# First blocks of a blocked triangular inverse: transposed on VectorE and moved by GpSimd instead of by TensorE products and ScalarE copies

## The reference, cut to what matters

```
def step(s, inp):
    r_t, w_t, k_t, v_t, kk_t, a_t = inp
    sa = jnp.einsum('bhvk,bhk->bhv', s, -kk_t)
    s = (s * w_t[:, :, None, :] + sa[..., None] * (kk_t * a_t)[:, :, None, :]
         + v_t[..., None] * k_t[:, :, None, :])
    return s, jnp.einsum('bhvk,bhk->bhv', s, r_t)
```

## Time and profile before

| | |
|---|---|
| Median of 3 runs | 3548.14 us (3544.28 to 3554.76) |
| Profiled execution | 3553.18 us, span 3551.4 us |
| PE, PEld, DVE, ACT, POOL busy | 3318.0, 2872.8, 2133.4, 766.6, 390.9 us |
| The scan's group loops | 181.4 to about 889 us, in four pieces (one for each pair) of about 108 us |
| L1109 and L1113, each | 36 times (4 pairs, 9 groups; pairs and groups are counted from 0) |

### The profile page before, as it was taken

How to read it: one execution, slowest core, us unless ns; L and a number is a source line. 1 busy time by engine, 2 the same in 40 slices (tenths; PEclk the granted TensorE clock), 3 DMA queues, 4 the chain that set the end, 5 groups by cost and what they waited for, 6 DMA issues and landing times.

```text
span 3551.4 us, 155986 instructions
## 1 busy us (share of the span) xinstructions
PE 3318.0 (93%) x72354; PEld 2872.8 (81%) x72354; DVE 2133.4 (60%) x3890; ACT 766.6 (22%) x1815; POOL 390.9 (11%) x536
## 2 busy tenths in 40 slices
PE   7989899898999999299999999999999999999997
PEld 3486767768455545299999999999999999999997
DVE  4566657676344444666666666666666665666665
ACT  3445344444244443000000000000000000000002
POOL 0141524334211000000000000000000000000001
PEclk9999999999999999699999999999999999999999
DMA  8200000000311113398989998988989989899996
GB/s 359 72 6 9 18 10 17 5 20 5 99 33 33 44 54 108 130 326 287 292 280 292 289 287 281 291 288 279 284 282 287 289 285 284 277 288 291 284 288 210
DMA packets 570778, 671.25 MB, mean 189 GB/s; under 512 B 56942, under 2 KB 463750, under 8 KB 567054
## 3 DMA queue, kind: packets, MB, share of 16 engines
q1 hardware_dynamic: 564430, 641.85, 55.5%
q0 software_dynamic: 5520, 19.34, 2.6%
q10 hardware_dynamic: 176, 0.05, 0.0%
HBM read 631.68 MB, written 28.30 MB: 186 GB/s over the span
## 4 chain that ended last, share of the span: by engine, by line
PE 56%; issue 1%; SPq 1%; DVE 1%; DMA 0%; ACT 0%; DVEq 0%
PE banks L2555 34%; PE banks L2580 20%; PE banks L2496 2%; SPq L2403 1%; SPq L2410 0%; DMA e_wgu<-in_e_up 0%; DVE e_wd L2859 0%; DVE e_wgu L2859 0%; SPq L2413 0%; DVE e_wgu L2928 0%; DVE e_xe L2917 0%; DVE e_wsum L2757 0%; ACT e_xp L2695 0%; ACT e_xT L2695 0%; DVE e_wgu L2762 0%
## 5 line engine op out<-in xcount | busy, mean ns | idle before, releaser
L2580 PE MATMUL banks<-e_hid,e_wd 128*64 128x144 f32 x11264 | 1280.4, 286 | 12.3 <-issue 9.5
L2580 PEld LDWEIGHTS banks<-e_hid,e_wd 128*64 128x64 f32 x11264 | 782.4, 137 | 15.6 <-issue 15.2
L2555 PE MATMUL banks<-e_xsum,e_wgu 128*64 128x72 f32 x11264 | 518.8, 226 | 12.2 <-issue 12.2
L2555 PE MATMUL banks<-e_xsum,e_wsum 128*64 128x72 f32 x11264 | 523.1, 226 | 7.2 <-issue 5.5
L2555 PE MATMUL banks<-e_xT,e_wgu 128*64 128x72 f32 x11264 | 519.1, 226 | 10.5 <-issue 9.2
L2555 PEld LDWEIGHTS banks<-e_xT,e_wgu 128*64 128x64 f32 x11264 | 501.3, 137 | 14.3 <-issue 14.2
L2555 PEld LDWEIGHTS banks<-e_xsum,e_wsum 128*64 128x64 f32 x11264 | 503.4, 137 | 8.9 <-issue 7.0
L2555 PEld LDWEIGHTS banks<-e_xsum,e_wgu 128*64 128x64 f32 x11264 | 498.7, 137 | 14.1 <-issue 14.0
L2790 DVE TENSOR_TENSOR e_gu<-e_first,banks 128x288 f32<-128x288 f32 x176 | 79.9, 454 | 676.2 <-ACT e_first L2676 507.5
L2676 ACT ACTIVATE e_first<-banks 128x144 f32<-128x144 f32 x176 | 51.4, 292 | 1416.4 <-PE banks L2555 1416.4
L2555 PE MATMUL banks<-e_xT,e_wsum 128*64 128x72 f32 x5632 | 257.7, 226 | 1.5 <-issue 1.3
(11 more groups left out here) (399 smaller groups left out, 4815.6 us busy)
## 6 DMA issues: line engine op xcount, KB each, us to landing
e_wgu<-in_e_gate SPq DMA_DIRECT2D x704, 256.0 KB
e_wgu<-in_e_up SPq DMA_DIRECT2D x704, 256.0 KB
e_wd<-in_e_down SPq DMA_DIRECT2D x704, 256.0 KB, 4.0
h_wmod<-in_w_mod SPq DMA_DIRECT2D x24, 1024.0 KB, 16.8
wblk<-in_w_in SPq DMA_DIRECT2D x22, 512.0 KB, 14.6
h_x<-in_x_sample SPq DMA_DIRECT2D x8, 512.0 KB, 7.1
wo<-in_w_out SPq DMA_DIRECT2D x2, 2048.0 KB, 11.9
scratch_ffn<-hT_x SPq DMA_DIRECT2D x8, 512.0 KB, 5.1
```

Source lines behind the costliest of these rows:

```text
L2555: last = nc.tensor.matmul(bank[4 + 2 * (n % 2) + g][c, q * HT:(q + 1) * HT], a[:, k, c], b[:, k, :], start=(k == 0), stop=(k == HALF - 1))
L2580: last = nc.tensor.matmul(bank[k // PER_BANK][c, at:at + TOK], wd[n % WD][:, b, k * P + h * CH:k * P + (h + 1) * CH], hid[n % 2][:, b, :], ...
```

## The change

PE's twelve products and ScalarE's two copies are gone. DVE's new `first_T(g)` makes the transposes, two `transpose` instructions of 128 x 128 that transpose each 32x32 block by itself; they stand in DVE's queue just ahead of `level(g, 1)`. The move to the other half is made by a masked sum that is written straight into the other half, twice 64 partitions: by GpSimd at the end of `first_inverse` for groups 1 to 8, by DVE in `inverse_start` for group 0. `w1_ok` counts these halves, and PE's `level_Y(g, 1)` waits for it.

```diff
-                    def inverse_start(g):
-                        pages.wait(w0_ok, p * GR + g + 1)
...
-                                    last = pages.matmul(bank[5][f, at:at + CH],
-                                                            W0[f, i, :] if d else TW[g % 2][f, d, 1, i, :],
-                                                            K.idc[f, :], start=True, stop=True)
-                        last.then_inc(t0ps, 1)
-                    def inverse_copy(g):
...
-                                last = pages.matmul(bank[6][HS[h], at:at + CH], K.idc[f, :], W0[f, i, :],
-                                                        start=True, stop=True)
-                        last.then_inc(w_cps, 1)
...
                             if d and lev == 1:
-                                pages.wait(w_cok, p * GR + g + 1)
+                                pages.wait(w1_ok, p * (2 * GR) + 2 * g + 2)
...
-                        act.wait_ge(t0ps, p * GR + g + 1)
...
-                        act.wait_ge(w_cps, p * GR + g + 1)
...
+                        pool.wait_ge(w0_ok, p * GR + g + 1)
+                        for h in range(2):
+                            f = FAR[1][h]
+                            nc.gpsimd.tensor_tensor(TW[g % 2][HS[h], 1, 1, :, :], N0[f, 1, :, :], eye[f], ALU.add)\
+                              .then_inc(w1_ok, 1)
+                            pool.wait_ge(w1_ok, p * (2 * GR) + 2 * g + h + 1)
...
+                        for h in range(2):
+                            f = FAR[1][h]
+                            V.tensor_tensor(TW[g % 2][HS[h], 1, 1, :, :], N0[f, 1, :, :], eye[f], ALU.add).then_inc(w1_ok, 1)
...
+                    def first_T(g):
+
+                        dve.wait_ge(w0_ok, p * GR + g + 1)
+                        for d in range(2):
+                            src = W0[:, :, :] if d else TW[g % 2][:, 0, 1, :, :]
+                            last = V.transpose(TW[g % 2][:, d, 0, :, :].rearrange("p i t -> p (i t)"),
+                                               src.rearrange("p i t -> p (i t)"))
+                        last.then_inc(t0_ok, 1)
...
                         if g < GR:
+                            first_T(g)
                             level(g, 1)
```

More of the change, by code:

```diff
@@ L560, in rwkv @@
         kvps, kv_ok = sem("PVKV_psum"), sem("PVKV_ok")
-        t0ps, t0_ok, tw_ok = sem("T0_psum"), sem("T0_ok"), sem("TW_ok")
+        t0_ok, tw_ok = sem("T0_ok"), sem("TW_ok")
         xps, x_ok, yps = sem("X_psum"), sem("X_ok"), sem("TW_psum")
@@ L568, in rwkv @@
         skd = sem("S_decayed")
-        w_cps, w_cok = sem("W_copy_psum"), sem("W_copied")
+        w1_ok = sem("W1_ok")
         w_in_v = A["w_in"].rearrange("l (k p) n -> p (l k) n", p=P)
@@ L948, in _ @@
                         j = 2 * (g - 1)
-                        if g == 0:
-                            inverse_start(0)
                         if g < GR:
                             level_X(g, 1)
-                            inverse_copy(g)
                         if g:
@@ L989, in _ @@
                             level_Y(g, 5)
-                        if g + 1 < GR:
-                            inverse_start(g + 1)
                 finish_first(PAIRS - 1)
@@ L1105, in v_major @@
                                   .then_inc(v_ok, 1)
-                    def inverse_start(g):
-                        act.wait_ge(t0ps, p * GR + g + 1)
-                        nc.scalar.activation(TW[g % 2][:, :, 0, :, :].rearrange("p d i t -> p d (i t)"),
-                                             bank[5][:, 2 * P:4 * P].rearrange("p (d n) -> p d n", d=2),
-                                             ACT.Copy).then_inc(t0_ok, 1)
-                        act.wait_ge(w_cps, p * GR + g + 1)
-                        nc.scalar.activation(TW[g % 2][:, 1, 1, :, :].rearrange("p i t -> p (i t)"),
-                                             bank[6][:, T_AT[1]:T_AT[1] + P], ACT.Copy).then_inc(w_cok, 1)
                     def state_U(j):
@@ L1152, in _ @@
                         j = 2 * (g - 1)
-                        if g < GR:
-                            inverse_start(g)
                         if g + 1 < GR:
@@ L1426, in added @@
                                 if d:
-                                    dve.wait_ge(w_cok, p * GR + g + 1)
+                                    dve.wait_ge(w1_ok, p * (2 * GR) + 2 * g + 2)
                             else:
```

## The result

The changed kernel took 3561.42 us (median of 10 runs, 3549.17 to 3571.66) against 3551.18 us before (10 runs, 3544.28 to 3557.57): 1.0032 of before, 95% interval 1.0017 to 1.0047, so about 10 to 11 us slower. I had forecast 3544 and 3533 to 3559 as its range.

A forecast was written before the change was run, and what follows sets the result against it. No engine is full, so the group loop is bound as a chain of waits. Terms sum to -1.0 us a pair, -4.0 in all: 3553.18 becomes 3549.1 profiled, and 3544 us as median, 5 us lower; range 3533 to 3559.

The forecast's parts named there:

- Price of the transposes: DVE's two transposes ahead of level 1: 0.49 us together, with bounds of 0.36 and 0.75 us.
- rival of dear transposes: Rival, 12%: DVE's two transposes take 0.90 us or more, making the kernel slower; 3562 us at 1.0 us a pair.
- GpSimd slowing them: Rival, 3%: GpSimd and VectorE slow each other; transposes tripled in 28 groups would give 3572 us.
- Level 1 behind DVE's last sum: Groups 3 to 8: PE's level 1 starts 0.46 us behind DVE's last sum instead of 0.62, -0.96 us a pair.
- Group 1: Start of level 1, now behind DVE's long L1498: +0.46 us from its end instead of -0.64, +1.10 us a pair.
- Group 2: Start of level 1, now behind DVE's long L1500: 0.46 us from its end instead of 0.00, +0.46 us a pair.
- Group 0: Level 1 about 1.14 us behind DVE's last masked sum instead of 2.35, -1.21 us a pair.
- The move: Four products moving W0 leave PE's queue behind level 1: 0.10 us won in groups 0 to 7, -0.80 us a pair.
- Page ends: PE's stalls at code page ends, 15 per pair for 16 but more on the chain: +0.4 us, bounds -0.5 and +1.5.
- GpSimd's cover: GpSimd's two 64-partition sums end about 1.1 us after L1211, some 3 us before `level_Y` needs them, so cost nothing.
- The sum: All terms of the four group loops together: -1.0 us per pair, times four -4.0 us.
- TensorE's clock falls (2%): Rival, 2%: with twelve products fewer ahead of a wait, the scan's products run at half clock; about 3600 us.

The follow-up runs named there:

- e1: Changed kernel with DVE's two long instructions moved behind state_Z of groups 1 and 2: 0.9991 of the kernel before; a repeat on another chip gave 0.9979.
- b1_before: The kernel before, unedited, run and profiled once more: profiled execution 3559.96 us, its four group loops summing to 471.8 us.
- e10: Changed kernel with eight unread products of constants behind the last level_Y of every group but the last: 1.0013 of the kernel before.
- e0: The changed kernel run again without any edit: 1.0034 of the kernel before.
- e3: Changed kernel with unread products of constants where PE's twelve stood, except in group 0: 1.0027 of the kernel before.
- e8: Changed kernel with unread products where PE's twelve stood (not in group 0) and DVE's two long instructions moved: 0.9993 of the kernel before.
- e11: Changed kernel with eight unread products behind the last level_Y of every group but the last, and DVE's long instructions moved: 0.9978 of the kernel before.

## Why the prediction was wrong

By its own steps:

- **Price of the transposes**: 0.49 us forecast for the two, 0.51 measured (193.62 to 194.13). They overlap, so the rival of dear transposes is out, and with a longest of 313 ns in 72 so is that of GpSimd slowing them. The Trainium skill (VectorE: DVE Perf Modes, The three transpose paths) gives 311 ns for bf16; the fp32 ones here took 304 and 268 ns.
- **Level 1 behind DVE's last sum**: 0.46 forecast, 0.47 measured in groups 3 to 8 of all pairs. Group 6 was counted as coming from 0.62 like the others, but it took 1.10 to 1.52 us in the profile of the kernel before, with a stall by issue of 0.31 to 0.73 us in PE's identity products: it won 0.8 us and not 0.16.
- **Group 1**: +1.10 forecast; it went from 0.62 to 1.86, +1.24. **Group 2**: +0.46 forecast; from a mean of 1.33 to 1.80, +0.47. Both right in kind and size; level 1 of group 1 is 0.59 us behind L1479's end, not 0.46, as the first transpose starts 0.03 us behind that end and not 0.08 ahead of it. What I didn't do was to ask what these 1.7 us a pair are beside the rest: e1 shows that the change with them moved away is faster than before, by 3 and by 7 us.
- **Group 0**: -1.21 forecast. From L1404 (L1372) to DVE's mask of level 1 it was 3.87 us on average and is 2.85, -1.02. A part is given back at once in a stall at the page end in M, the first line of the fence below.
- **The move**: -0.10 forecast; 1.38 to 1.28 us from level 1 to `level_Y`, -0.10.
- **Page ends**: +0.4 forecast. The sum of stalls is unchanged (34.7 for 34.3). Two that now stand on the path are plain in the changed kernel's loads, the second in all four pairs:

```profile
182.56 0.14 PEld L159 LDWEIGHTS banks<-r_QR,r_K 64*64 64x64 f32 x2 [1.27 <-issue]
...
190.69 0.20 PEld L159 LDWEIGHTS banks<-r_TW,r_M 64*64 64x64 f32 x4 [0.46 <-issue]
```

The first is the page end of M, 0.39 to 1.27 us (in the first profile of before, 0.22 at most in the same place; in the one of b1_before once 0.39), the second lies in level 5, where before the page ended in the products of PV. No run takes this step apart from the others.
- **GpSimd's cover**: its two sums were to end 1.1 us after L1211 and did (614.92, 1.06 us behind L1173's end, pair 2). L1190 starts 0.90 us later, 0.81 us ahead of PE's level 1, where it was 0.88 before. For 21 of its waits the profile names L1178 and not ScalarE as what came last, so that sign failed, but nothing waits longer for it.
- **The sum**: -1.0 us a pair forecast; the groups without a fall give -1.1, from 113.5 to 112.4. As long as the clock held, the sum stood as forecast. That it is so close is in part luck: group 6 won 0.6 us more than its term, and the eight pairs of before differ by up to 2.1 us.
- **The step that failed** is the rival "TensorE's clock falls (2%)", which the likeliest case put at nothing. The wait it named was foreseen (2 us at groups 1 and 2; 2.3 came), but I let the clock stand at 1.00 on rows with waits of 0.6 us, gave the fall 2%, and priced it as all or nothing ("about 3600"). What came is eight or nine falls more of 3.4 us each, at 1.2 us. That is about 10 us, against -4 for the rest: +6, where the three comparisons measured 10, 12 and 6. The falls were always there in the changed kernel, with the mean clock 0.977 in both repeats.

What is left over the +6, from nothing to 6 us, isn't assigned. The price of a fall rests on the same groups with and without one, not on a kernel that mends the clock and nothing else: e10 mended half of it and won 1 us of the 4 to be expected, inside the uncertainty, with 7.4 us more of issue waits. What is shown by removal is the queue: three pairs of runs (e0 and e1, e3 and e8, e10 and e11) give 12 to 15 us for taking the long instructions out of the way. Since that also shortens PE's waits, in the first of them a part of the 15 is falls (8.8 more than before with them, 5.4 without).

So the change acted on the clock through PE's waits. The eight transposing products stood in the wait between DVE's last sum and level 1 and left 0.6 us of it; without them it is 0.94 us, and 2.3 behind the long instructions.

## What to carry to other kernels

When an edit takes products from an engine that also waits, look at what those products did to the waits around them: here eight of PE's twelve stood in a wait, and with them gone and the transposes queued behind DVE's long instructions the clock fell some eight times a run, as the granted clock of a profile shows. When work is moved to another engine, list what is already queued there at that place; two instructions of 1.4 us that cost nothing before cost 11 us as soon as something on the path stood behind them, and moving them into a place where DVE waits anyway made the same change a gain of 0.1 to 0.2%. And fill a wait with unread products only after counting what they cost: here they brought the clock back and no time.

## What was not expected of the hardware

- A fall of the granted clock took 3.4 us in each case in the scan (or twice that), and cost this loop 1.2 us on average.
- Falls came behind waits of 0.9 us too (e1: at 230, 459 and 616 us), though rarely: at 20 of 185 boundaries, against 25 of 32 with waits of 2.3 us and 1 of 328 with waits up to 0.70.
- GpSimd's sums over 64 partitions take 451 ns, as those over 128 do (0.46 us); half the partitions save nothing.
